# An mLSTM on one core: another division of the PSUM banks, another order of the projections, and an output gate by tanh

## The reference

```
(sb, scg, sx, mq, mk, mv, mo, mg, dq, dk, dv, gs, gm, gd) = split_cols(u @ w_in + b_in)
y_sc = sb * centred_depthwise_conv(scg * sx, conv_w)
m_t = jnp.maximum(m_inter, jnp.max(d_log, axis=-1))        # the stabiliser
s = jnp.einsum('bhtd,bhsd->bhts', qc, kc) * jnp.exp(d_log - m_t[..., None])
h_out = num / jnp.maximum(jnp.abs(den), jnp.exp(-m_t))[..., None]
y_ml = jax.nn.sigmoid(mo) * from_heads(hl_ml)
y = (sigmoid(gs) * (y_sc @ w_sc) + sigmoid(gm) * (y_ml @ w_ml) + sigmoid(gd) * (y_da @ w_da)) @ w_o
```

## Time and profile before

| | |
|---|---|
| median of three runs | 2512.01 us (2511.97 to 2513.91) |
| profiled execution, its own time | 2512.22 us |
| its span | 2510.4 us |
| TensorE busy (matmul) | 2441.2 us, 97% |
| VectorE busy | 1556.0 us, 62% |
| ScalarE busy | 1086.3 us, 43% |
| DMA, share of the 16 engines | 43.6% |

### The profile page before, as it was taken

The page is one execution under the profiler, slowest core; times in us unless marked ns, Lnnn a source line. Parts: engine busy times, 40 slices in busy tenths (PEclk is TensorE's granted clock), DMA queues, the critical chain, the costliest instruction groups (busy, mean ns, idle before and its releaser), DMA issues.

```text
span 2510.4 us, 36016 instructions
## 1 busy us (share of the span) xinstructions
PE 2441.2 (97%) x13138; PEld 2073.5 (83%) x13138; DVE 1556.0 (62%) x2541; ACT 1086.3 (43%) x2075; POOL 0.2 (0%) x4
## 2 busy tenths in 40 slices
PE   7999999999999999999999999999999999998998
PEld 3888888887778778898888888888888888998998
DVE  2577687546445454567775467776666555667666
ACT  3434334534433434354343254333345454555555
POOL 0000000000000000000000000000000000000000
PEclk9999999999999999999999999999999999999999
DMA  6466453332222322316663326664433433554654
GB/s 236 145 190 184 129 168 114 85 92 68 59 67 69 93 76 72 103 54 209 187 183 104 93 80 184 184 184 138 135 89 102 115 102 94 160 144 136 200 164 121
DMA packets 519489, 320.69 MB, mean 128 GB/s; under 512 B 13974, under 2 KB 481344, under 8 KB 519360
## 3 DMA queue, kind: packets, MB, share of 16 engines
q1 hardware_dynamic: 517912, 318.59, 43.6%
q10 hardware_dynamic: 1448, 0.38, 0.1%
HBM read 317.87 MB, written 1.05 MB: 127 GB/s over the span
## 4 chain that ended last, share of the span: by engine, by line
PE 86%; DVE 6%; ACT 5%; issue 3%; DMA 0%; SPq 0%; DVEq 0%; ACTq 0%
PE ps L771 24%; PE ps L773 24%; PE ps L772 24%; PE ps L1005 2%; ACT w_hi L1156 2%; PE ps L830 1%; DVE w_lo L1608 1%; PE ps L831 1%; PE ps L832 1%; PE ps L758 1%; PE ps L740 1%; PE ps L1022 1%; PE ps L1041 1%; ACT h L1214 1%; ACT u_hi L1205 0%
## 5 line engine op out<-in xcount | busy, mean ns | idle before, releaser
L1608 DVE TENSOR_TENSOR w_lo<-raw,w_hi 128x1024 fp32r<-128x1024 f32 (+1 forms) x446 | 534.5, 1199 | 614.0 <-ACT w_hi L1156 611.1
L771 PE MATMUL ps<-u_hi,w_hi 128*128 128x512 f32 (+1 forms) x2368 | 862.7, 364 | 0.2 <-DVE w_lo L1608 0.2
L1156 ACT ACTIVATE w_hi<-raw 128x1024 fp32r<-128x1024 f32 (+1 forms) x446 | 462.7, 1037 | 902.2 <-PE ps L773 808.5
L773 PE MATMUL ps<-u_hi,w_lo 128*128 128x512 f32 (+1 forms) x2368 | 848.1, 358 | 0.0
L772 PE MATMUL ps<-u_lo,w_hi 128*128 128x512 f32 (+1 forms) x2368 | 847.1, 358 | 0.0
L773 PEld LDWEIGHTS ps<-u_hi,w_lo 128*128 128x128 f32 x2368 | 447.2, 189 | 66.5
L772 PEld LDWEIGHTS ps<-u_lo,w_hi 128*128 128x128 f32 x2368 | 447.9, 189 | 64.0 <-issue 1.0
L771 PEld LDWEIGHTS ps<-u_hi,w_hi 128*128 128x128 f32 x2368 | 447.6, 189 | 63.8 <-issue 1.3
L771 PE MATMUL ps<-g_hi,w_hi 128*128 128x512 f32 (+1 forms) x770 | 271.9, 353 | 1.1 <-DVE w_lo L1608 1.0
L772 PE MATMUL ps<-g_lo,w_hi 128*128 128x512 f32 (+1 forms) x770 | 269.3, 350 | 0.0
L773 PE MATMUL ps<-g_hi,w_lo 128*128 128x512 f32 (+1 forms) x770 | 269.2, 350 | 0.0
(11 more groups left out here) (254 smaller groups left out, 2767.4 us busy)
## 6 DMA issues: line engine op xcount, KB each, us to landing
raw<-in_ffn_up SPq DMA_DIRECT2D x154, 512.0 KB, 3.8
raw<-in_w_in SPq DMA_DIRECT2D x132, 512.0 KB, 3.8
ada_in_up<-in_w_ada SPq DMA_DIRECT2D x108, 512.0 KB, 3.9
raw<-in_ffn_down SPq DMA_DIRECT2D x64, 384.0 KB, 3.4
raw<-in_ffn_down SPq DMA_DIRECT2D x48, 320.0 KB, 3.1
h<-in_ffn_up SPq DMA_DIRECT2D x22, 512.0 KB, 3.9
ada_in_down<-in_w_ada SPq DMA_DIRECT2D x20, 512.0 KB, 4.0
stage<-in_w_ada SPq DMA_DIRECT2D x16, 512.0 KB, 10.6
```

Source lines behind the costliest of these rows:

```text
L771: pe.matmul(ps[bank][:, cols_of], wh, a_hi, start=a, stop=False)
L773: m = pe.matmul(ps[bank][:, cols_of], wl, a_hi, start=False, stop=b)
L1156: act.activation(split_tiles(w_hi, slot)[:, 0:kn, :], raw_tiles(raw_slot, kn), ACT.Copy).then_inc(hi_done, 1)
L1608: dve.tensor_tensor(split_tiles(w_lo, slot)[:, 0:kn, :], raw_tiles(place[0], kn), split_tiles(w_hi, slot)[:, 0:kn, :].bitcast(F32), ALU.su ...
```

## The change

One edit is a new list of steps. Before, a head had six places for projections: behind two scores, behind the other two, behind the first numerator, behind a pair, behind the last numerator, and behind the transpose. Now it has five: two behind all four scores, one behind numerators 0 and 1, one behind numerators 2 and 3, one behind the transpose. 20 projections stand there instead of 23, and 9 instead of 6 behind the heads. `vector_order` is gone.

The banks are divided anew. Projections 16 to 38 of a layer alternate between banks 0 and 1. The four scores of a head take banks 6, 7, 2 and 3, the numerators 6 and 7 for even and 2 and 3 for odd t. The waits follow: a score waits for no `pw` any more, a numerator only for the `hs` two steps back, a projection for the last one in its own bank.

The spread multiplies 64 rows instead of 128: the backward stabiliser is put at rows 64 to 95, and each direction has a matmul of its own half of the rows. The output gate is a tanh of half the argument; 1 is added as it is multiplied, and the factor 0.5 goes to the copies of `ht` and to the bias, which is halved at the start of the kernel like that of the other gates.

```diff
@@ proj_order @@
-    fill = [(kind, i) for i in range(4) for kind in ("cg", "sx", "sb")]
-    fill += [("dq", 0), ("dk", 0)] + [("mo", i) for i in range(4)] + [("dq", 1), ("dk", 1), ("dq", 2), ("dk", 2)]
-    fill += [("mo", 4), ("mo", 5), ("dv", 0), ("dv", 1)]
-    order += [fill.pop(0), ("turn_v", 7), fill.pop(0), ("ml_gates", 0), fill.pop(0)]
+    conv = [(kind, i) for i in range(4) for kind in ("cg", "sx", "sb")]
+    order += [conv.pop(0), ("turn_v", 7), conv.pop(0), ("ml_gates", 0), conv.pop(0)]
+    fill = conv + [("dq", 0), ("dk", 0)] + [("mo", i) for i in range(4)]
+    fill += [(kind, i) for i in range(1, 4) for kind in ("dq", "dk")][:-1]
     for h in range(HEADS):
-        for group in ([("ml_s", h, 0), ("ml_s", h, 1)], [("ml_s", h, 2), ("ml_s", h, 3)], [("ml_n", h, 0)],
-                      [("ml_n", h, 1), ("ml_n", h, 2)], [("ml_n", h, 3)], [("ml_t", h)]):
-            order += group + fill[:1]
-            del fill[:1]
+        for group, n in ([("ml_s", h, s) for s in range(TT)], 2), ([("ml_n", h, 0), ("ml_n", h, 1)], 1), \
+                ([("ml_n", h, 2), ("ml_n", h, 3)], 1), ([("ml_t", h)], 1):
+            order += group + fill[:n]
+            del fill[:n]
...
+    order += [("dk", 3), ("rope", 0), ("rope", 4)]
+    order += [("mo", 4), ("rope", 1), ("rope", 5), ("ysplit", 0)]
+    order += [("mo", 5), ("rope", 2), ("rope", 6), ("ysplit", 1)]
+    order += [("mo", 6), ("rope", 3), ("rope", 7), ("ysplit", 2)]
+    order += [("dv", 0), ("ysplit", 3), ("mo", 7), ("ysplit", 4)]
...
+BESIDE_ML = range(16, 39)
...
+PROJ_BANK = [n % (2 if n in BESIDE_ML else 4) for n in range(CH_PROJ)]
+SCORE_ML = (6, 7, 2, 3)
+NUMERATOR = ((6, 7), (2, 3))
@@ TensorE, proj @@
+                earlier = [m for m in range(n) if PROJ_BANK[m] == PROJ_BANK[n]]
+                pe.wait_ge(*proj_done(layer, earlier[-1]))
+                if n > BESIDE_ML[-1]:
+                    pe.wait_ge(hsum_ready, nth_out(layer, HEADS - 1, TT - 1) + 1)
@@ TensorE, ml_scores @@
-                    row = 32 * n + head
-                    m = pe.matmul(ps[4 + n][:, t0:TOK], ident[:, row:row + 1].to_broadcast([P, P]),
-                                  neg_g[:, t0:TOK], start=True, stop=True)
+                    own, row = slice(64 * n, 64 * n + 64), 64 * n + head
+                    m = pe.matmul(ps[4 + n][:, t0:TOK], ident[own, row:row + 1].to_broadcast([64, P]),
+                                  neg_g[own, t0:TOK], start=True, stop=True)
...
-            else:
-                if s >= 2:
-                    pe.wait_ge(pw_ready, 8 * u + 2 * (s - 1))
@@ TensorE, ml_numerator @@
-            if t > first:
-                pe.wait_ge(hsum_ready, nth_out(layer, head, t))
+            if t > first + 1:
+                pe.wait_ge(hsum_ready, nth_out(layer, head, t) - 1)
@@ ScalarE @@
-                dst, func = scr[i % 2][:, t0:TOK], ACT.Sigmoid
+                dst, func = scr[i % 2][:, t0:TOK], ACT.Tanh
...
-                m = act.activation(ht[:, 2 * head + e, t0:TOK], ps[4 + e][:, t0:TOK], ACT.Copy)
+                m = act.activation(ht[:, 2 * head + e, t0:TOK], ps[4 + e][:, t0:TOK], ACT.Copy, scale=0.5)
@@ VectorE @@
-                dve.tensor_tensor(ht[:, i, t0:TOK], scr[i % 2][:, t0:TOK], ht[:, i, t0:TOK], ALU.mult
-                                  ).then_inc(yf_ready, 1)
+                dve.scalar_tensor_tensor(ht[:, i, t0:TOK], scr[i % 2][:, t0:TOK], 1.0, ht[:, i, t0:TOK],
+                                         ALU.add, ALU.mult).then_inc(yf_ready, 1)
...
-                dve.memset(neg_g[64:128, :], 0.0)
+                dve.memset(neg_g[32:64, :], 0.0)
+                dve.memset(neg_g[96:128, :], 0.0)
```

More of the change, by code:

```diff
@@ L550, in nth_out, with proj_done @@
         return (HEADS * TT if layer else 0) + n * head + max(0, t - (TT - n))
+    def proj_done(layer, n):
+        kind, i = NTH_PROJ[n]
+        _, _, a, d = PLANS[layer][kind, i]
+        _, a0, d0 = BASES[layer, "proj"]
+        return (evac_act, a0 + a + 1) if EVAC_ENGINE[kind] == "act" else (evac_dve, d0 + d + 1)
     def gate_temp(step):
@@ L559, in gate_free @@
         if n < 4:
[L560 to L563, removed]
+            return proj_done(layer, CH_PROJ - 4 + n)
         step = GATE_CHUNKS[layer][n - 4]
@@ L913, in proj @@
             if n >= 4:
-                last = NTH_PROJ[n - 4]
-                by = EVAC_ENGINE[last[0]]
-                _, _, a, d = PLANS[layer][last]
-                pe.wait_ge(evac_act if by == "act" else evac_dve, (a0 + a if by == "act" else d0 + d) + 1)
-                chunk(base + r, (base + r) % SPLIT, n % 4, of(u_hi, u_lo, range(KD), t), t)
+                earlier = [m for m in range(n) if PROJ_BANK[m] == PROJ_BANK[n]]
+                pe.wait_ge(*proj_done(layer, earlier[-1]))
+                if n > BESIDE_ML[-1]:
+                    pe.wait_ge(hsum_ready, nth_out(layer, HEADS - 1, TT - 1) + 1)
+                chunk(base + r, (base + r) % SPLIT, PROJ_BANK[n], of(u_hi, u_lo, range(KD), t), t)
             elif n == 3:
@@ L978, in ml_scores @@
                 wait(pe, hsum_ready, nth_out(layer, head, 0))
-            else:
-                if s >= 2:
-                    pe.wait_ge(pw_ready, 8 * u + 2 * (s - 1))
             ts = max(t0, SEG if s >= 2 else 0)
-            pe.matmul(ps[6 + s % 2][:, ts:TOK], kt[:, head, s * P:(s + 1) * P], qt[:, head, ts:TOK],
+            pe.matmul(ps[SCORE_ML[s]][:, ts:TOK], kt[:, head, s * P:(s + 1) * P], qt[:, head, ts:TOK],
                       start=True, stop=True).then_inc(s_ready, 1)
@@ L1004, in ml_numerator @@
                 for s in keys:
-                    m = pe.matmul(ps[6 + n][:, 0:257], pw[:, n, s, t * P:(t + 1) * P], vaug[:, s, head, :],
+                    m = pe.matmul(ps[NUMERATOR[t % 2][n]][:, 0:257], pw[:, n, s, t * P:(t + 1) * P], vaug[:, s, head, :],
                                   start=(s == keys[0]), stop=(s == keys[-1]))
@@ L1682, in halved_biases @@
             for layer in range(DEPTH):
-                ct, cc = bias_at(layer, SEC["gs"])
-                own = cols[:, ct, cc:cc + 3 * KD]
-                link(dve.tensor_scalar(own, own, 0.5, None, ALU.mult))
+                for kind, n in (("mo", KD), ("gs", 3 * KD)):
+                    ct, cc = bias_at(layer, SEC[kind])
+                    own = cols[:, ct, cc:cc + n]
+                    link(dve.tensor_scalar(own, own, 0.5, None, ALU.mult))
         def lambdas():
@@ L1990, in proj @@
             t0 = t0_of(layer, kind in X_ONLY)
-            bank = ps[n % 4]
+            bank = ps[PROJ_BANK[n]]
             ahead(base, r)
@@ L2115, in ml_numerator @@
                 dve.wait_ge(gate_act, 5 * layer + 5)
-            nt = nth_out(layer, head, t)
+            nt, num = nth_out(layer, head, t), [ps[b] for b in NUMERATOR[t % 2]]
             dve.wait_ge(num_ready, nt + 1)
             for n in range(2):
-                m = dve.tensor_scalar(small[:, 12 + n:13 + n], ps[6 + n][:, 256:257], -1.0, None, ALU.mult)
+                m = dve.tensor_scalar(small[:, 12 + n:13 + n], num[n][:, 256:257], -1.0, None, ALU.mult)
             link(m)
@@ L2224, in mixer @@
             t0 = t0_of(layer)
-            for step in vector_order(ORDERS[layer]):
+            for step in ORDERS[layer]:
                 if step[0] in EVAC_ENGINE:
```

28 lines of the change are left out of this document (10 added, 18 removed).

## The result

The changed kernel takes 2516.66 us (median of 20 runs, 2515.27 to 2521.84); the kernel before, timed in turn with it on the same chips, 2513.38 (2511.33 to 2514.74). The ratio is 1.0016, 95% interval 1.001 to 1.0023: the kernel is a little slower, by 3.3 us (2.5 to 5.8 by the interval), where the prediction asked for 5 us to call it a change. The time is 3.7 us above the forecast of 2513.0 and inside its own range. The forecast was +0.75 us on an execution of 2512.22; the kernel before turned out at 2513.38, so as a difference it is 2.5 us short. The profiled execution has a span of 2514.9 us for 2510.4.

A forecast was written before the change was run, and what follows sets the result against it. TensorE, busy 2441.2 of 2510.4 us, was taken as the bound, with 18 us of waits recoverable. Terms -2.0 - 0.6 + 0.8 + 1.95 + 0.6 = +0.75 us on 2512.22 gave 2513.0; own range 2509 to 2517, whole range 2507 to 2519.5.

The forecast's parts named there:

- The clock: TensorE in the heads of both layers and layer 1's tail: granted clock kept at 1.00, 2.4 GHz.
- Layer 0, waits after: Heads of layer 0: transposes wait for `hs` behind VectorE's projection work; 12.6 us lost against 11.8, +0.8.
- Layer 1, waits after: Heads of layer 1: mainly bank waits of 1.65 and 3.8 us in heads 0 and 1; 6.7 against 4.75, +1.95.
- tail: Behind layer 1's heads: TensorE waits for banks 6 and 7 at the rotations, 2.0 us against 1.4, +0.6.
- Spread: Pairs of 64-row spread matmuls in the heads partly overlap: 1.25 us for 1.72 at 512 columns, -2.0 in all.
- Fewer breaks: Layer 0 has four groups of float32 work between projections per head for six, 0.07 us each: -0.6.
- Tanh: ScalarE's table loads among the heads go; their waits in heads 2 already counted, otherwise off the path: no further gain.
- the 18 us: All that TensorE's waits in both layers' heads and layer 1's tail can give back, 0.7%.
- rival 1: The two banks hurt every head of layer 1: about 6 us slower, 2519; chance 0.22.
- rival 2: Layer 1 has no bank wait: sum -4.7 us, 2507.5, or 2506 with a shorter `hs` wait; chance 0.12.
- rival 3: Spread row tiles run in parallel without overhead: -5.2 us for -2.0, 2509.8; chance 0.12.
- A, B and C: Projections of each head: the first two stand behind the four scores, the third behind the first two numerators.

The follow-up runs named there:

- experiment 6: The changed kernel with extra discarded matmuls filling TensorE's waits for `hs` in the heads of layer 0: 2515.61 us, ratio 1.0008.
- experiment 1: The changed kernel, but VectorE takes the first numerator of each pair ahead of the projection in front of it: 2505.54 us, ratio 0.9966.
- experiment 2: The changed kernel, but ScalarE and VectorE take each head's first projection between scores 1 and 2, in both layers: 2513.73 us, ratio 1.0002.
- experiment 4: The kernel before with the spread from 64 rows alone: 2513.74 us, ratio 1.0.
- experiment 5: The kernel before with the output gate by tanh alone: 2506.53 us, ratio 0.9972.
- Experiment 7: The kernel before with the new banks and their waits alone; old order, sigmoid and 128-row spread stay: 2502.83 us, ratio 0.9955.
- Experiment 9: The changed kernel with VectorE's numerator exchange in both layers and the earlier first projection in layer 1 alone: 2499.99 us, ratio 0.995.
- experiment 8: The kernel before with new banks, 64-row spread and tanh, on the old order of steps: 2492.93 us, ratio 0.9917.

## Why the prediction was right, and what its sum lacked

"The same" was right, and the mechanism too: the old bank waits went, new waits of the forecast kind and size came in their places. Of the terms:

- **The clock.** "The granted clock is 1.00 in all three, the level of 2.4 GHz, and I keep it there" is the step that failed. It is 1.7 us in layer 0 (shown by experiment 6, and by 1) and 1.5 in layer 1 (gone with the wait in experiment 2). Without it the stretches are -2.2 and +2.5 us; forecast were -1.7 (waits +0.8, spread -1.9, breaks -0.6) and +2.45 (waits +1.95 and +0.6, spread -0.1). With it the sum of the two is +3.5, and the medians moved by 3.3. The half clock near the norms, +2.9 and -1.2 in the traces, was not in the sum either, and the medians don't show it.
- **Layer 0, waits after, +0.8.** Forecast 12.6 lost; the five rows have 11.4, and with 0.15 for each it is 12.2. Head by head they lie within 0.35 us.
- **Layer 1, waits after, +1.95, and tail, +0.6.** C's waits were 1.51 and 3.31 for 1.65 and 3.8. The one for `ht` was 0.86 for 0.9; that for `hs` 1.08 for 0.35. With 0.15 for each the four lose 7.4 for 6.7. The rotations waited 1.3 and not 2.0 us, 1.6 with the 0.15. Against 4.75 and 1.4 before, that makes +2.6 and +0.2. The two misses offset each other to 0.3 us, which is luck.
- **Spread, -2.0.** 0.47 a head at 512 columns, to the hundredth (experiment 4). The 0.39 us above one matmul isn't one drain: 0.2 of it lies ahead of the pair and behind it, and 0.2 in the pair. The Trainium skill, TensorE: Matmul & The Clock Gate, section on packing small matmuls, has tiles side by side cost hardly more than one; here a pair cost 1.25 us where one matmul takes 0.86, so the row decides. Alone on the old banks it gave 1.0 us in layer 0, and in the medians nothing that can be told.
- **Fewer breaks, -0.6.** No experiment takes this term alone.
- **Tanh, "otherwise off the path".** It holds: the waits that tanh removes were in the 18 us, and as the prediction says they are those of heads 2, which hold 6.0 of the 6.4 us of experiment 5. What it did not say is how much that is, about a third of the 18. Experiment 7, with the banks and without tanh, still waits 4.3 us there.
- **Rivals.** Banks in every head of layer 1 (rival 1): only heads 0 and 1 waited. No bank wait (rival 2): it waited. Row tiles without overhead (rival 3): 1.25 us a pair, not 0.86.

What no step of mine weighed was the order by itself. I priced the new order and new banks together, at about nothing, and they are: banks, spread and tanh gain 20.7 us together, and the order takes 24 back. Of these 10.6 are shown to be B standing on VectorE ahead of the numerators whose `hs` TensorE wants (experiment 1), and 4.4 in layer 1 to be A evacuated late while A, B and C follow each other with two banks for three (experiment 2). Experiment 9 mends both and still stays 7.7 us behind experiment 8 in the layers; most of that is waits for `hs` and `pw`, the rest is open.

## What to carry to other kernels

When a change gives buffers and reorders work at once and the time hardly moves, split it: here the buffers with the cheap edits were worth 20.7 us, and the order took 24 back. Where an engine gets two instructions in a row for which it needs something from another, look at what that other engine has queued between them; an exchange of two steps on VectorE was worth 11 us. Price a wait of some microseconds on TensorE with the slower matmuls behind it, and an activation function from another table with two loads in the middle of the chain that it interrupts.
